# Attention outputs with 128 value columns, and one PSUM bank for each head

## The reference

```
mla:  16 heads, q and k of 64 + 32 columns, v of 64
      p = softmax(causal(q k^T * scale));  out = p v
dsa:  16 heads of 64 in 4 key/value groups; keys chosen by top-256 of an index score
      p = softmax(q k^T / 8 + bias[bucket] + mask);  out = p v
fox:  8 heads of 64
      p = softmax(causal(q k^T / 8 + F[t] - F[s]));  out = p v
```

## Time and profile before

| | us |
|---|---|
| median of 3 runs | 2430.2 |
| lowest and highest | 2420.52, 2444.06 |
| profiled execution | 2422.34 |
| its span | 2420.5 |

### The profile page before, as it was taken

How to read it: one execution, slowest core, us unless ns; L and a number is a source line. 1 busy time by engine, 2 the same in 40 slices (tenths; PEclk the granted TensorE clock), 3 DMA queues, 4 the chain that set the end, 5 groups by cost and what they waited for, 6 DMA issues and landing times.

```text
span 2420.5 us, 47668 instructions
## 1 busy us (share of the span) xinstructions
PE 2317.2 (96%) x18858; PEld 2134.7 (88%) x18862; DVE 1246.4 (51%) x2504; ACT 1010.3 (42%) x1555; POOL 160.8 (7%) x186
## 2 busy tenths in 40 slices
PE   7999999999999989889999999999989998999998
PEld 7966899899999978756899989999969787999997
DVE  5467344455553146999453455553154644656412
ACT  4556254243332143756353343332153535555413
POOL 1000100100000040135100100000030000000000
PEclk9999999999999999899999999999999999999999
DMA  6333242344552222100242235543212202333220
GB/s 161 82 74 83 83 146 69 87 112 132 137 149 99 102 63 70 37 19 1 70 157 70 71 105 136 150 130 122 87 44 87 76 18 70 89 103 96 95 104 35
DMA packets 307592, 219.02 MB, mean 90 GB/s; under 512 B 42698, under 2 KB 294544, under 8 KB 307472
## 3 DMA queue, kind: packets, MB, share of 16 engines
q1 hardware_dynamic: 255792, 189.30, 26.2%
q10 hardware_dynamic: 49920, 25.17, 4.0%
q0 software_dynamic: 1760, 2.88, 0.4%
HBM read 207.56 MB, written 2.10 MB: 87 GB/s over the span
## 4 chain that ended last, share of the span: by engine, by line
PE 90%; ACT 5%; DVE 3%; issue 1%; DMA 0%; POOL 0%; SPq 0%; DVEq 0%; ACTq 0%; POOLq 0%
PE bank L637 72%; PE bank L779 5%; PE bank L749 3%; PE bank L713 3%; PE bank L879 1%; PE bank L1094 1%; PE bank L937 1%; PE bank L929 1%; ACT ST L1510 1%; PE bank L1143 1%; ACT XH L1180 1%; ACT XT L1354 1%; ACT BI L1180 1%; DVE SC L1963 1%; ACT WH L600 0%
## 5 line engine op out<-in xcount | busy, mean ns | idle before, releaser
L637 PE MATMUL bank<-XH,WH 128*128 128x256 f32 x3568 | 1003.3, 281 | 33.0 <-DVE XL L1828 24.4
L637 PE MATMUL bank<-XL,WH 128*128 128x256 f32 x3568 | 996.7, 279 | 0.0
L637 PE MATMUL bank<-XH,WL 128*128 128x256 f32 x3568 | 996.5, 279 | 0.0
L637 PEld LDWEIGHTS bank<-XH,WH 128*128 128x128 f32 x3568 | 678.7, 190 | 41.9 <-issue 32.1
L637 PEld LDWEIGHTS bank<-XH,WL 128*128 128x128 f32 x3568 | 676.1, 189 | 0.0
L637 PEld LDWEIGHTS bank<-XL,WH 128*128 128x128 f32 x3568 | 675.1, 189 | 0.2 <-issue 0.2
L604 DVE TENSOR_TENSOR WL<-RAW,WH 128x2048 fp32r<-128x2048 f32 x172 | 394.2, 2292 | 525.8 <-ACT WH L600 525.8
L600 ACT ACTIVATE WH<-RAW 128x2048 fp32r<-128x2048 f32 x172 | 328.6, 1911 | 445.7 <-PE bank L637 445.5
L637 PE MATMUL bank<-HH,WH 128*128 (+1 forms) x1056 | 295.2, 280 | 0.9 <-DVE HF L1908 0.9
L637 PE MATMUL bank<-HH,WL 128*128 (+1 forms) x1056 | 294.9, 279 | 0.0
L637 PE MATMUL bank<-HL,WH 128*128 (+1 forms) x1056 | 294.9, 279 | 0.0
(11 more groups left out here) (304 smaller groups left out, 3168.3 us busy)
## 6 DMA issues: line engine op xcount, KB each, us to landing
RAW<-in_ffn_w_in SPq DMA_DIRECT2D x88, 512.0 KB, 5.0
MB<-in_mod_w ACTq DMA_DIRECT2D x48, 512.0 KB, 5.2
RAW<-in_ffn_w_down SPq DMA_DIRECT2D x44, 512.0 KB, 3.9
RAW<-in_ffn_up SPq DMA_DIRECT2D x44, 512.0 KB, 4.5
RAW<-in_xa_w_kv SPq DMA_DIRECT2D x32, 512.0 KB, 4.4
RAW<-in_ffn_down SPq DMA_DIRECT2D x22, 512.0 KB, 4.0
RAW<-in_xa_w_q SPq DMA_DIRECT2D x16, 512.0 KB, 4.0
RAW<-in_xa_w_o SPq DMA_DIRECT2D x16, 512.0 KB, 4.4
```

Of the source, the lines that this page charges most:

```text
L637: mm = nc.tensor.matmul(out_ap[:, cols], l, moving, start=(start and n == 0 and k == 0), stop=(stop and n == len(parts) - 1 and k == len(o ...
```

## The change

The output matmuls of mla, dsa and fox take 128 value columns, those of both heads of a pair. For each head this gives 128 rows, of which the 64 of that head are used. Even heads write bank 6 and odd heads bank 7, and each head's 64 rows are evacuated alone, after four steps. In dsa, where four heads share their values, an odd head needs its group's values in columns 64 to 127 of the block: it takes the block that begins one group to the left, and VK gets a fifth block of 64 columns, a copy of the first. In mla the values of a pair are staged by one DMA. Two semaphores for the even heads are added.

```diff
-        VK = at("VK", [P, NQ, 256], region + 19 * KB)
+        VK = at("VK", [P, NQ, 320], region + 18 * KB)
...
+        def head_rows(hh):
+            return slice(64 * (hh % 2), 64 * (hh % 2) + 64)
+
+        EVEN0 = {"mla_o": 1, "fox_o": 1 + HEADS // 2}
...
-                        if not first:
-                            sp.wait_ge(av_done, g * 16 + (STEP0["mla"] - 16 + 4 * hh + 4))
-                        sp.dma_start(V_M[:, :, NOPE * hh:NOPE * hh + NOPE],
-                                     VM[:, :, bass.ds(g * 256 + NOPE * hh, NOPE)]).then_inc(values_staged[hh], 16)
+                        if hh % 2:
+                            if not first:
+                                sp.wait_ge(av_done, g * 16 + (STEP0["mla"] - 16 + 4 * hh + 4))
+                            pair = hh // 2
+                            sp.dma_start(V_M[:, :, P * pair:P * pair + P],
+                                         VM[:, :, bass.ds(g * 256 + P * pair, P)]).then_inc(values_staged[pair], 16)
...
                     hh, qb = divmod(i, 4)
-                    o = bank[6 + hh // 2 % 2][64 * (hh % 2):64 * (hh % 2) + 64, P * qb:P * qb + P]
+                    o = bank[6 + hh % 2][:, P * qb:P * qb + P]
...
-            def o_split(fill):
+            def o_split(fill, odd0):
                 def o_free(pe, g, i):
-                    if i in (0, 8):
-                        pe.wait_ge(x_split, g * 2 + (FILL0[fill] + i // 8 - 1))
+                    if i % 8 == 0:
+                        pe.wait_ge(even_split, g * 2 + (EVEN0[fill] + i // 8))
+                    elif i % 8 == 4:
+                        pe.wait_ge(x_split, g * 2 + (odd0 + i // 8))
                 return o_free
...
+            def pair_of_heads(values):
+                return lambda hh, kb: values[:, kb, P * (hh // 2):P * (hh // 2) + P]
+            attention("mla", 4, 4, mla_logits, head_av("mla", pair_of_heads(V_M)), o_split("mla_o", FILL0["mla_o"]),
+                      mla_staged)
...
             def dsa_o_free(pe, g, i):
-                if i % 8 == 0:
-                    pe.wait_ge(o_copied, i // 8 + 1)
+                if i % 4 == 0:
+                    pe.wait_ge(o_copied, i // 4 + 1)
+
+            def dsa_values(hh, kb):
+
+                left = 64 * (hh // 4) if hh % 2 == 0 else 64 * ((hh // 4 - 1) % 4)
+                return VK[:, kb, left:left + P]
...
-                    elif i % 8 == 7:
+                    elif i % 4 == 3:
                         act.wait_ge(av_done, g * steps + (s0 + i + 1))
-                        out_tile(g, i // 8)
+                        out_tile(g, i // 4)
...
+            def head_hi(g, hh):
+                r = head_rows(hh)
+                copy(XH[r, bass.ds(g * 2 + hh // 2, 1), :], bank[6 + hh % 2][r, :]).then_inc(x_hi if hh % 2 else even_hi, 1)
...
-            copy(VK[:, :, :], VD[:, :, :]).then_inc(v_moved, 1)
+            copy(VK[:, :, 0:256], VD[:, :, :])
+            copy(VK[:, :, 256:320], VD[:, :, 0:64]).then_inc(v_moved, 1)
...
-            def o_copy(g, k):
-                copy(QD[:, k, :], bank[6 + k % 2][:, :]).then_inc(o_copied, 1)
+            def o_copy(g, hh):
+                r = head_rows(hh)
+                copy(QD[r, hh // 2, :], bank[6 + hh % 2][r, :]).then_inc(o_copied, 1)
...
+            def head_lo(fill, hi0):
+                def out_tile(g, hh):
+                    r, pair = head_rows(hh), bass.ds(g * 2 + hh // 2, 1)
+                    if hh % 2:
+                        dve.wait_ge(x_hi, g * 2 + (hi0 + hh // 2 + 1))
+                    else:
+                        dve.wait_ge(even_hi, g * 2 + (EVEN0[fill] + hh // 2))
+                    nc.vector.tensor_tensor(XL[r, pair, :], bank[6 + hh % 2][r, :], f32(XH[r, pair, :]),
+                                            ALU.subtract).then_inc(x_split if hh % 2 else even_split, 1)
+                return out_tile
```

More of the change, by code:

```diff
@@ L334, in build_program @@
         keys_padded = sem("keys_padded")
-        values_staged = [sem(f"values_staged{hh}") for hh in range(4)]
+        values_staged = [sem(f"values_staged{pair}") for pair in range(2)]
         bias_staged = sem("bias_staged")
@@ L339, in build_program @@
         o_copied = sem("o_copied")
+        even_hi = sem("even_hi")
+        even_split = sem("even_split")
         idx_ready = sem("idx_ready")
@@ L893, in mla_staged @@
                         pe.wait_ge(head_staged[i // 4], g * 48 + 48)
[L894 to L897, removed]
+                    elif i % 8 == 0:
+                        pe.wait_ge(values_staged[i // 8], g * 16 + 16)
+            def pair_of_heads(values):
+                return lambda hh, kb: values[:, kb, P * (hh // 2):P * (hh // 2) + P]
+            attention("mla", 4, 4, mla_logits, head_av("mla", pair_of_heads(V_M)), o_split("mla_o", FILL0["mla_o"]),
+                      mla_staged)
             wide_stage("mla_o", xpairs(), "mla_o", behind=memory_turn(0))
@@ L1101, in dsa_o_free @@
             def dsa_o_free(pe, g, i):
-                if i % 8 == 0:
-                    pe.wait_ge(o_copied, i // 8 + 1)
+                if i % 4 == 0:
[3 more added lines that the diff above has]
+                return VK[:, kb, left:left + P]
             pe.wait_ge(keys_padded, 2)
             pe.wait_ge(bias_free, BIAS_CREDIT + 40)
-            attention("dsa", 1, 16, dsa_logits, head_av("dsa", lambda hh, kb: VK[:, kb, 64 * (hh // 4):64 * (hh // 4) + 64]),
-                      dsa_o_free, dsa_staged)
+            attention("dsa", 1, 16, dsa_logits, head_av("dsa", dsa_values), dsa_o_free, dsa_staged)
             wide_stage("dsa_o", xpairs(), "dsa_o", behind=memory_turn(1))
@@ L1146, in fox_logits @@
                                         start=False, stop=True)
[L1148 to L1152, removed]
+            attention("fox", 1, 8, fox_logits, head_av("fox", pair_of_heads(VF)), o_split("fox_o", FILL0["fox_o"] + 4),
+                      not_staged)
             wide_stage("fox_o", xpairs(), "fox_o", (4, 5, 6, 7, 0, 1, 2, 3))
@@ L1300, in attention, with o_hi @@
                 pipeline(act, groups, steps, 3 if xa else 4, 0, tick)
[L1302 to L1305, removed]
+            def o_hi(g, k):
+                copy(XH[:, k, :], bank[4 + k % 4][:, :]).then_inc(x_hi, 1)
+            def head_hi(g, hh):
+                r = head_rows(hh)
+                copy(XH[r, bass.ds(g * 2 + hh // 2, 1), :], bank[6 + hh % 2][r, :]).then_inc(x_hi if hh % 2 else even_hi, 1)
             log_exp_tables()
-            attention("mla", 4, 4, MLA_SCALE, o_hi("mla_o"))
+            attention("mla", 4, 4, MLA_SCALE, head_hi)
             def wide_units(name, per_unit, pairs=None):
@@ L1407, in cross_attention @@
                 wide_units(q, queries)
-                attention(f"xa{layer}", 1, 4, (D // 4) ** -0.5, o_hi(f"xa{layer}_o", 4, 4))
+                attention(f"xa{layer}", 1, 4, (D // 4) ** -0.5, o_hi)
                 for i in range(4):
@@ L1539, in _ @@
             for c in range(DC):
-                act.wait_ge(o_copied, 2 + 8)
+                act.wait_ge(o_copied, 2 + HEADS)
                 if c == 0:
@@ L1607, in _ @@
             after_unit("fox_pool", 0, 0, TILE0["fox_pool"] + 4)
-            attention("fox", 1, 8, 0.125, o_hi("fox_o"))
+            attention("fox", 1, 8, 0.125, head_hi)
             wide_units("fox_o", nothing)
@@ L1623, in _ @@
                 dve.sem_inc(s, 4)
+            dve.sem_inc(even_split, 1)
             nc.vector.memset(VR[:, :, :], 0.0).then_inc(cols_done, 1)
@@ L1759, in attention, with o_lo @@
                 pipeline(dve, groups, steps, 4 if xa else 5, LAG, tick)
-            def o_lo(fill, hi0, b0=6, banks=2):
+            def o_lo(fill, hi0):
                 def out_tile(g, k):
-                    dve.wait_ge(x_hi, g * 2 + (hi0 + k + 1))
-                    c = g * 2 + k
-                    nc.vector.tensor_tensor(XL[:, bass.ds(c, 1), :], bank[b0 + k % banks][:, :], f32(XH[:, bass.ds(c, 1), :]),
+                    dve.wait_ge(x_hi, hi0 + k + 1)
+                    nc.vector.tensor_tensor(XL[:, k, :], bank[4 + k % 4][:, :], f32(XH[:, k, :]),
                                             ALU.subtract).then_inc(x_split, 1)
+                return out_tile
[8 more added lines that the diff above has]
+                                            ALU.subtract).then_inc(x_split if hh % 2 else even_split, 1)
                 return out_tile
@@ L1770, in x_hi0 @@
                 return FILL0[fill] - 8
-            attention("mla", 4, 4, MLA_SCALE, lambda g, i: cm(i % 4), o_lo("mla_o", x_hi0("mla_o")))
+            attention("mla", 4, 4, MLA_SCALE, lambda g, i: cm(i % 4), head_lo("mla_o", x_hi0("mla_o")))
             def proj_units(stage, gain=None, split_last=True, between=None):
@@ L1873, in cross_attention @@
                 attention(f"xa{layer}", 1, 4, (D // 4) ** -0.5, lambda g, i: KC[:, K_CM:K_CM + MEM],
-                          o_lo(f"xa{layer}_o", x_hi0(f"xa{layer}_o"), 4, 4))
```

(3 more changed lines are left out.)

## The result

| | before | changed |
|---|---|---|
| median of 4 runs each | 2428.1 us | 2397.0 us |
| lowest and highest | 2420.5, 2444.1 | 2390.5, 2408.4 |
| profiled execution, its span | 2422.3, 2420.5 | 2390.5, 2388.7 |

The ratio is 0.9886 with a 95% interval of 0.9853 to 0.992. So the changed kernel is faster by 0.8 to 1.5%. The forecast was 2401 us. The two medians lie 31.1 us apart, a little more than the ratio says (1.14%, 27.7 us); both lie inside the interval, which goes from 19 to 36 us.

What follows compares the result with a forecast made beforehand. PE, busy 96% of the span, was taken to bound the kernel, with DVE and POOL setting dsa. Savings of 17.3 + 8.1 + 0.4 - 0.3 = 25.5 us from 2426.3 gave 2401 us, range 2385 to 2424.

Steps and rivals of the forecast that it cites:

- The gap of 0.29 us a step in mla, 17.3 us: PE in mla: switches between 64 and 128 weight columns go, 18.1 us less 0.8 for first steps and tail.
- fox, 8.1 us: PE in fox: the same switches go, 8 x 1.13 = 9.0 us less 0.9 for start and tail.
- dsa, 0.4 us, behind DVE and POOL: dsa: switch gain hidden behind DVE; only the tail and waits ahead of key copies give 0.4 us, bounds 0 and 18.1.
- Evacuations for each head, free: mla and fox: one ACT copy (0.59 us) and DVE subtraction (0.69) more a pair, covered under PE's 5.48 us a head.
- Banks, staging: Banks coming back after one head and mla values staged by two DMAs instead of four: costs nothing.
- VK, 0.3 us: Wider VK in dsa: a second ACT copy of 256 elements costs 0.3 us ahead of the bias steps, bounds 0 and 0.5.
- The sum: Whole kernel: 17.3 + 8.1 + 0.4 - 0.3 = 25.5 us saved; from the middle of the runs, 2426.3, to 2401 us.
- The first: Rival in dsa: PE, not DVE, sets its pace, so another 17.7 us go, 2383 us; 7 in 100.
- the second: Rival in mla and fox: DVE or ACT takes over, a head may take 6.1 us, 2414 us; 15 in 100.
- the third: Rival: gaps come from something else at group borders and stay; costs 1.5 us, 2428 us; 8 in 100.
- The fourth, slower through wide passes: Rival in mla, fox, dsa: a wide pass costs what two narrow ones do, 2467 us; 3 in 100.
- The column tiling that the prediction set beside it: Argument against widening: 64-column weights suit column tiling, twice as fast at best, which widening would forfeit; result as last rival.

Runs made afterwards that it cites:

- e8: The changed kernel measured again unchanged, beside the kernel before on the same chip; 2400.4 us, ratio 0.9887.
- e1: Changed kernel with its banks, evacuations, staging and VK kept, but output matmuls of 64 weight columns into the head's own 64 rows; 2420.9 us.
- e2: Changed kernel with 64 weight columns in the output matmuls of even heads only, 128 for odd heads; 2415.1 us.
- e6: Changed kernel with POOL's bias sums in dsa cut to 32 columns and DVE's maximum taking the causal mask instead; 2377.7 us, dsa 93.7.
- e3: Changed kernel with each output matmul of 128 weight columns issued as two of 64 on the two halves of the array; 2427.5 us.
- e7: Changed kernel with the normalisation of dsa's 128-key steps moved from DVE to ACT as a scaled copy; 2385.6 us, ratio 0.9828 to the kernel before.
- e9: Kernel of e7 with the odd half of each later dsa key copy moved from DVE to ACT; 2386.3 us, ratio 0.9839.
- e4: Changed kernel with 96 weight columns in the output matmuls of even heads, 128 for odd heads; 2395.0 us.

## Why the prediction was right

- *The gap of 0.29 us a step in mla, 17.3 us.* Right: 17.7 in the first profile, 18.4 in e8. The price of the dense head, 5.48 us, came from the cross attention's passes; the head is 5.49. e1 gives 17.2 of it back, e2 half.
- *fox, 8.1 us.* 7.7. The head went from 7.16 to 6.08, 1.08 instead of 1.13, eight times, and the start loses what I took off.
- *dsa, 0.4 us, behind DVE and POOL.* 1.0, and 0.8 in e8. The mechanism is shown by e6, where the hidden part appears. Of the 1.0, 0.5 are DVE's waits ahead of the key copies, which go, 0.2 the tail, and 0.3 the start, which e8 hardly has. Two things in the reading were loose. DVE did not set dsa alone: PE's 6.62 ran between the copies, and DVE's limit lay 1.4% under it. And 16 x 6.52 + 3 x 1.27 = 108 us is not the stretch's length: fifteen heads take 101.3 us from DVE's first 512-wide maximum to its last, and another 12.5 lie ahead of them and behind.
- *Evacuations for each head, free.* The half rows cost what I took, the whole: 0.58 and 0.69 us in the groups by form. DVE rose to 90% in mla, and PE's head stayed at 5.49 until 188 us. e1 shows no cost either, but at a head of 6.62; wide passes with one evacuation a pair were not run. Behind that a head takes up to 5.6, and from 205 us on the chain of the changed kernel passes over DVE's maximum: there the cover is gone, for a few tenths of a us. The groups by form of ACT and DVE in mla (145 to 220 us; count, busy us, mean ns, idle):

```profile
L1195 ACT ACTIVATE XH<-bank 64x512 f32 x12 | 7.0, 584 | 0.1
...
L1795 DVE TENSOR_TENSOR XL<-bank,XH 64x512 f32 x12 | 8.3, 689 | 1.1 <-issue 0.3
```

- *Banks, staging.* At most 0.5 us, as e1 shows for all of them together.
- *VK, 0.3 us.* The second copy takes 0.40 us; ACT's next stage began 3.16 us behind the first copy's start, 2.85 before. The instructions that write VK (ns min/median/max, first and last start):

```profile
L1195 ACT ACTIVATE VK<-VD x2: 403/724/1046, 970.2 to 971.1; 128x1024 f32<-128x1024 f32 x1, 128x256 f32<-128x256 f32 x1
```

- *The sum.* 25.5 us against 26.4 and 27.0. Held to the middle of the runs it gave 2401; the median is 2397.0. That these two lie so near is partly luck: the runs of the changed kernel spread over 18 us, and the medians differ by 31.1 us, 5.6 more than the sum. What bears the sum out is the stretches.
- *Rivals.* The first fell with dsa's 1.0 us, the second with the 5.49 us head, the third with e1 against the changed kernel. The fourth, slower through wide passes, fell: 0.111 us a pass. The column tiling that the prediction set beside it does work (e3): two narrow passes can run side by side. It took nothing away here because the kernel before never had the two halves at work together; its heads' outputs followed each other in time.
- *Why not more.* The change shortens PE by 40 x 1.1 = 44 us; 16 x 1.1 = 18 of them lie in dsa, where DVE with POOL was already as slow. e7 and e9, which shorten DVE's side of it, took 14 us off dsa.

## What to carry to other kernels

Compare starts of PE's groups with the same helper at another shape in the same trace: what is lost at the borders shows in no duration, and a matmul of 64 weight columns between ones of 128 lost 0.29 us each time it came and went. Use the other 64 columns even for work that is thrown away. Or put real work on both halves; it would have to be in longer groups than e3's, where the borders ate the gain (no run here has such groups). Before you count a saving on PE, look for the engine that is nearly as slow in that stretch, since two limits within 2% of each other make either saving nearly worthless alone.

## What the runs showed of the hardware

- Narrow weights beside wide ones: 0.09 us into the narrow group and 0.05 in it, 0.09 out and 0.05 behind, at the full granted clock; 96 columns beside 128 cost nothing (e4).
- Two narrow matmuls on the two halves of the columns run at once: 16 passes in 1.03 us, where 8 take 1.02 (e3).
- The load of a wide block of values takes 192 ns against 137 for a narrow one, but the pass interval is 0.111 against 0.109 us. The width alone is not the reason: the transposes' loads, of 128 columns too, take 140 ns.
- The normalisation on DVE beside a POOL sum of 1.27 us takes 1.23 us; the same form takes 0.29 in mla, without POOL, and in dsa with the sums cut (e6). With the sums cut, DVE's busy time in dsa falls from 96% to 82% at a head of 5.48 in place of 6.52.
- Whole projection stages run at 0.113 or 0.118 us a pass in different executions of one kernel (e8). Between the two profiles of the changed kernel that makes 15 us; the other runs have no trace that would show it.
